# Two schedules of a two-block decoder kernel: the convolution stage projected by tokens, and the differential attention's steps behind later pieces

## The reference, cut to what matters

```python
def _odd_layer(h, w_in, conv_w, w_out, rows):          # convolution layer, width 4096 inside
    bg, cg, xt, g = jnp.split(h @ w_in, 4, axis=-1)    # w_in: 2048 x 16384
    y = bg * _conv3(cg * xt, conv_w, rows) * jax.nn.silu(g)
    return y @ w_out
# _conv3: three taps along each row of 64 tokens, zero at the row's ends
```

## Time and profile before

| | |
|---|---|
| runs | 2790.6, 2791.35 (median), 2792.13 us |
| profiled execution | 2791.76 us, its span 2790.1 us |
| busy share of the span | TensorE 96%, weight loads 90%, VectorE 63%, ScalarE 46%, GpSimd 1% |
| chain that ended last | TensorE 80%, VectorE 8%, ScalarE 4%, DMA 4%, VectorE's queue 3% |
| DMA | 534.59 MB, mean 192 GB/s |
| convolution stage | about 1847 to 2592 us of the span |
| differential attention | about 444 to 662 us, its last steps to 701 us |

### The profile page before, as it was taken

The page is one execution under the profiler, slowest core; times in us unless marked ns, Lnnn a source line. Parts: engine busy times, 40 slices in busy tenths (PEclk is TensorE's granted clock), DMA queues, the critical chain, the costliest instruction groups (busy, mean ns, idle before and its releaser), DMA issues.

```text
span 2790.1 us, 47619 instructions
## 1 busy us (share of the span) xinstructions
PE 2682.4 (96%) x18449; PEld 2500.2 (90%) x18449; DVE 1749.9 (63%) x2260; ACT 1278.6 (46%) x1702; POOL 18.4 (1%) x33
## 2 busy tenths in 40 slices
PE   7999999998899799999999999999999999999997
PEld 7999889998888699999989988889999999999886
DVE  6868878786875755545557545566775555555644
ACT  5557444555545444434443344444454444444443
POOL 1000000000000000000000000000000000000000
PEclk9999999999999899999999999999999999999999
DMA  6565866764566455655568645547875555556553
GB/s 190 147 200 167 277 185 197 221 204 142 187 213 213 155 179 173 194 163 184 175 194 265 205 144 181 191 152 235 282 256 183 180 187 174 188 173 195 175 201 138
DMA packets 450706, 534.59 MB, mean 192 GB/s; under 512 B 32955, under 2 KB 343750, under 8 KB 449670
## 3 DMA queue, kind: packets, MB, share of 16 engines
q1 hardware_dynamic: 447840, 522.29, 58.5%
q0 software_dynamic: 2064, 10.11, 1.2%
q10 hardware_dynamic: 662, 0.25, 0.0%
HBM read 530.46 MB, written 2.10 MB: 191 GB/s over the span
## 4 chain that ended last, share of the span: by engine, by line
PE 80%; DVE 8%; ACT 4%; DMA 4%; DVEq 3%; issue 1%; SPq 1%; ACTq 0%
PE banks L1802 15%; PE banks L1804 14%; PE banks L1803 14%; PE banks L1813 10%; PE banks L1814 10%; PE banks L1815 10%; DVE w_lo L1197 3%; DMA w_raw<-in_ev_w_in 2%; ACT w_hi L673 1%; PE banks L2195 1%; DVEq L1188 1%; PE banks L1965 1%; ACT scr_a L794 1%; DMA w_raw<-in_od_w_in 1%; SPq L492 1%
## 5 line engine op out<-in xcount | busy, mean ns | idle before, releaser
L1197 DVE TENSOR_TENSOR w_lo<-w_raw,w_hi 128x1024 fp32r<-128x1024 f32 (+2 forms) x848 | 974.4, 1160 | 744.2 <-ACT w_hi L673 723.1
L673 ACT ACTIVATE w_hi<-w_raw 128x1024 fp32r<-128x1024 f32 (+2 forms) x848 | 842.8, 1005 | 1012.4 <-PE banks L1815 394.6
L1802 PE MATMUL banks<-act_hl,w_hi 128*128 128x256 f32 x4048 | 1169.3, 289 | 37.5 <-DVE w_lo L1197 14.2
L1803 PE MATMUL banks<-act_hl,w_hi 128*128 128x256 f32 x4048 | 1149.9, 284 | 0.0
L1804 PE MATMUL banks<-act_hl,w_lo 128*128 128x256 f32 x4048 | 1149.7, 284 | 0.0
L1802 PEld LDWEIGHTS banks<-act_hl,w_hi 128*128 128x128 f32 x4048 | 780.4, 193 | 53.9 <-issue 21.7
L1803 PEld LDWEIGHTS banks<-act_hl,w_hi 128*128 128x128 f32 x4048 | 781.0, 193 | 1.9 <-issue 0.7
L1804 PEld LDWEIGHTS banks<-act_hl,w_lo 128*128 128x128 f32 x4048 | 780.5, 193 | 0.0
L1813 PE MATMUL banks<-w_hi,act_hl 128*128 128x512 f32 (+3 forms) x1376 | 510.5, 371 | 7.9 <-DVE w_lo L1197 5.7
L1814 PE MATMUL banks<-w_lo,act_hl 128*128 128x512 f32 (+3 forms) x1376 | 509.8, 370 | 0.0
L1815 PE MATMUL banks<-w_hi,act_hl 128*128 128x512 f32 (+3 forms) x1376 | 508.7, 370 | 0.0
(11 more groups left out here) (275 smaller groups left out, 1643.7 us busy)
## 6 DMA issues: line engine op xcount, KB each, us to landing
w_raw<-in_od_w_in SPq DMA_DIRECT2D x256, 512.0 KB, 3.9
w_raw<-in_ev_w_in SPq DMA_DIRECT2D x256, 256.0 KB, 3.8
w_raw<-in_l_w_in SPq DMA_DIRECT2D x96, 512.0 KB, 4.3
w_raw<-in_l_w_in SPq DMA_DIRECT2D x128, 256.0 KB, 3.2
ada_ring<-in_ada_w SPq DMA_DIRECT2D x128, 256.0 KB, 4.3
w_raw<-in_l_w_out SPq DMA_DIRECT2D x64, 512.0 KB, 5.0
y_mix<-in_ada_w SPq DMA_DIRECT2D x128, 256.0 KB, 3.3
const_b<-in_ada_w SPq DMA_DIRECT2D x128, 256.0 KB, 4.8
```

The source lines that it names most:

```text
L673: last = nc.scalar.activation(dst(w_hi[:, p % RING, :]), src(w_raw[:, p % RING, :]), ACT.Copy)
L1197: last = tt(dst(w_lo[:, p % RING, :]), src(w_raw[:, p % RING, :]), dst(w_hi[:, p % RING, :]).bitcast(F32), ALU.subtract)
L1802: mm(out, hi, a[:, kt, 0:T], start=start, stop=False, skip_group_check=True)
L1803: mm(out, hi, a[:, kt, T:2 * T], start=False, stop=False, skip_group_check=True)
```

## The change

The convolution stage is projected by tokens: banks 0 and 1 take [c | g] of token tile 0 and 1, banks 2 and 3 [b | x], each in matmuls of 512 columns whose moving operand is two blocks of 256 weight columns. Behind piece 2 ScalarE copies c and takes Silu of g for both token tiles; VectorE then multiplies banks 2 and 3 by them, which gives b times the gate and x times c by tokens. Behind piece 3 TensorE turns both products to features in eight transposes, into banks 4 and 5. Behind piece 8 VectorE applies the taps from bank 5, skipping the row ends in place of a zero border, and multiplies by bank 4. The `mix_pair` steps move from 8 to 10, and in out3 the last ones from 7 to 8. In differential attention the exponentials are cut into two heads behind piece 7 and two behind piece 8; the normalisation goes from 8 to 9, the transposes from 7 to 8, probT's copy from 10 to 11, the values from 9 to 10, the square from 12 to 13, its sum from 11 to 12, the root from 14 to 15. VectorE's steps behind 6, 14 and 15 stay.

```diff
@@ -308,7 +308,7 @@
     "four": ("gate", "folded", "cols", "cols_sb", "rows", "rows_sb", "o", "y"),
-    "conv": ("y",),
+    "conv": ("prod", "turned", "y"),
 }.items():
@@ -543,9 +543,8 @@
 four_e, four_o = view(scr_b[:, 1536:1792], 2, P), view(scr_b[:, 1792:2048], 2, P)
-conv_x, conv_g, conv_b, conv_y = (scr_b[:, 512 * n:512 * n + 512] for n in range(4))
-conv_c = scr_b[:, 2576:3088]
-conv_z = scr_b[:, 2048:2576].rearrange("p (b r n) -> p b r n", b=2, r=4)
+conv_gc, conv_prod = view(scr_b[:, 0:1024], TT, 512), view(scr_b[:, 1024:2048], TT, 512)
+conv_y = scr_b[:, 2048:2560]
 gate_rows = scr_b[:, 2560:4608]
@@ -860,17 +859,19 @@
             nc.scalar.activation(at_g, at_g, ACT.Silu).then_inc(s["gate"], 1)
-        if p == 6:
+        if p == 7:
             sc.wait_ge(s["max"], i + 1)
-            exps(dif_s, range(4), s["exp"])
-        if p == 10:
+            exps(dif_s, (0, 1), s["exp"])
+        if p == 8:
+            exps(dif_s, (2, 3), s["exp"])
+        if p == 11:
             sc.wait_ge(s["probT"], i + 1)
             copy(view(dif_t, 2, 384), PS[:, 4:6, 0:384]).then_inc(s["probT_sb"], 1)
-        if p == 12:
+        if p == 13:
             sc.wait_ge(s["o"], i + 1)
...
             nc.scalar.activation(dif_sq, bank(6), ACT.Square).then_inc(s["sq"], 1)
-        if p == 14:
+        if p == 15:
             sc.wait_ge(s["mean"], i + 1)
@@ -955,15 +956,12 @@
         if p == 2:
-            sc.wait_ge(s["y"], i + 1)
-            full(sc, "conv", i, 1)
-            copy(conv_b, bank(A)).then_inc(s_free, 1)
-            full(sc, "conv", i, 2)
-            copy(conv_x, bank(B)).then_inc(s_free, 1)
-            full(sc, "conv", i, 3)
-            copy(conv_c, bank(C)).then_inc(s_free, 1)
-            full(sc, "conv", i, 4)
-            nc.scalar.activation(conv_g, bank(3), ACT.Silu).then_inc(s_free, 1)
+            sc.wait_ge(s["prod"], i + 1)
+            for t in range(TT):
+                full(sc, "conv", i, 1 + t)
+                copy(conv_gc[:, t, T:2 * T], PS[:, t, 0:T])
+                last = nc.scalar.activation(conv_gc[:, t, 0:T], PS[:, t, T:2 * T], ACT.Silu)
+                last.then_inc(s_free, 1)
@@ -1129,7 +1127,7 @@
             conv(p, i)
-            if p == 8:
+            if p == 10:
                 mix_pair(i - 8)
@@ -1143,7 +1141,7 @@
             4: mixes("out3", 10),
-            7: [y_ready("conv"), *mixes("out3", 11)],
+            8: [y_ready("conv"), *mixes("out3", 11)],
             12: [lambda: gate_rows_copy(2)]}))
@@ -1429,8 +1427,8 @@
             scores_max(dif_s, range(4), causal, 4, s["max"])
-        if p == 8:
-            ve.wait_ge(s["exp"], i + 1)
+        if p == 9:
+            ve.wait_ge(s["exp"], 2 * i + 2)
@@ -1521,25 +1519,29 @@
         s = S["conv"]
-        if p == 3:
-            ve.wait_ge(s_free, all_left("conv", i))
+        if p == 2:
+            ve.wait_ge(s_free, bank_count("conv", i, 2))
+            ve.wait_ge(s["turned"], i + 1)
+            for t in range(TT):
+                full(ve, "conv", i, 3 + t)
+                last = tt(conv_prod[:, t, :], PS[:, 2 + t, :], conv_gc[:, t, :], ALU.mult)
+                last.then_inc(s_free, 1)
+            drain().then_inc(s["prod"], 1)
+        if p == 8:
+
+            ve.wait_ge(s["turned"], i + 2)
             rows = "p (b r n) -> p b r n"
-            z, v = conv_z, conv_y.rearrange(rows, b=2, r=4)
-            tt(z[:, :, :, 1:65], conv_c.rearrange(rows, b=2, r=4), conv_x.rearrange(rows, b=2, r=4),
-               ALU.mult)
-            drain()
-            for tap in (1, 0, 2):
+            z, v = PS[:, 5, :].rearrange(rows, b=2, r=4), conv_y.rearrange(rows, b=2, r=4)
+            for tap, src, dst in ((1, (0, 64), (0, 64)), (0, (0, 63), (1, 64)), (2, (1, 64), (0, 63))):
                 for b in range(2):
                     w = pcol(CONV3_W, 32 * tap + 2 * i + b)
-                    zs = z[:, b, :, tap:tap + 64]
+                    zs, vs = z[:, b, :, src[0]:src[1]], v[:, b, :, dst[0]:dst[1]]
                     if tap == 1:
-                        ts(v[:, b, :, :], zs, w, None, ALU.mult)
+                        ts(vs, zs, w, None, ALU.mult)
                     else:
-                        stt(v[:, b, :, :], zs, w, v[:, b, :, :], ALU.mult, ALU.add)
+                        stt(vs, zs, w, vs, ALU.mult, ALU.add)
                 drain()
-            tt(conv_y, conv_y, conv_b, ALU.mult)
-            drain()
-            tt(yt[:, ds(2 * i, 2), :], halves(conv_y), halves(conv_g), ALU.mult).then_inc(s["y"], 1)
+            tt(yt[:, ds(2 * i, 2), :], halves(bank(4)), halves(conv_y), ALU.mult).then_inc(s["y"], 1)
@@ -1580,6 +1582,8 @@
         ve.sem_inc(S[stage]["y"], 1)
+    for name in ("prod", "turned"):
+        ve.sem_inc(S["conv"][name], 1)
@@ -1690,10 +1694,6 @@
         norm(*norm5, range(4))
-
-    def clear_borders():
-        nc.vector.memset(conv_z, 0.0)
-        drain()
@@ -1770,9 +1770,9 @@
             conv(p, i)
-            if p == 8:
+            if p == 10:
                 mix_pair("out3", i - 8)
-        split("conv")(0, placed({**norm_steps(last_block, *norm5), 8: [clear_borders]}))
+        split("conv")(0, placed(norm_steps(last_block, *norm5)))
         for first, end in LOOPS["conv"][1:]:
@@ -1780,9 +1780,10 @@
             1: [lambda: mix_pair("out3", KT // 2 - 1)],
-            2: [step(conv, 3, COUNT["conv"] - 1), *mixes("out3", 8, 9)],
+            2: [step(conv, 2, COUNT["conv"] - 1), *mixes("out3", 8, 9)],
             4: mixes("out3", 10),
-            7: mixes("out3", 11),
+            6: [step(conv, 8, COUNT["conv"] - 1)],
+            8: mixes("out3", 11),
             9: [lambda: gate_diags(2, 80)]}))
@@ -1946,11 +1947,12 @@
+        blocks = [w[:, slot, 0:1024].rearrange("p (a b n) -> p b a n", a=2, b=2) for w in (w_hi, w_lo)]
         for b in range(4):
...
                 enter(stage, i, 1 + b)
-            for q in range(2):
-                r = features(half(b, q), slot, 256 * b + q * P, act, p, first and q == 0, last)
+            hi, lo = (w[:, 1 - b // 2, :, :] for w in blocks)
+            r = tokens_of(bank(b), hi, lo, act, p, b % 2, first, last)
             if last and b < 3:
@@ -2115,17 +2117,17 @@
             sets_scores(pairs, 4).then_inc(s["scores"], 1)
-        if p == 7:
+        if p == 8:
             te.wait_ge(s["prob"], i + 1)
...
             transposes([v[:, h, 0, :] for h in range(2)], 4).then_inc(s["probT"], 1)
-        if p == 9:
+        if p == 10:
             te.wait_ge(s["probT_sb"], i + 1)
...
             r.then_inc(s["o"], 1)
-        if p == 11:
+        if p == 12:
             te.wait_ge(s["sq"], i + 1)
@@ -2233,6 +2235,20 @@
+    def conv(p, i):
+        s = S["conv"]
+        if p == 3:
+
+            te.wait_ge(s["prod"], i + 2)
+            te.wait_ge(s["y"], i + 1)
+            for part in range(2):
+                for t in range(TT):
+                    for q in range(2):
+                        c = part * T + q * P
+                        r = nc.tensor.transpose(PS[:, 4 + part, q * T + t * P:q * T + (t + 1) * P],
+                                                conv_prod[:, t, c:c + P], ident[:, :])
+            r.then_inc(s["turned"], 1)
+
     def gates_rows(n):
@@ -2310,9 +2326,10 @@
         norm(5, x, first_columns, lambda: te.wait_ge(s_added, COUNT["out2"]))
-        stage_loop(te, "conv", run("conv"), none, nothing)
+        stage_loop(te, "conv", run("conv"), conv, nothing)
     if wanted("out3"):
-        stage_loop(te, "out3", run("out3"), none, placed({11: [lambda: gates_rows(2)]}))
+        n = COUNT["conv"] - 1
+        stage_loop(te, "out3", run("out3"), none, placed({3: [step(conv, 3, n)], 11: [lambda: gates_rows(2)]}))
```

## The result

| | us | ratio to the kernel before |
|---|---|---|
| before, beside it | 2790.97 (4 runs, 2790.11 to 2792.13) | |
| changed | 2761.21 (4 runs, 2759.15 to 2761.80) | 0.989 [0.9878, 0.9902] |
| predicted | 2757.5 (range 2752 to 2779) | |

The account below looks back on a forecast made before the run. The prediction took the convolution stage as bound by TensorE's issue and differential attention by TensorE with small holes. Convolution -27.9 and attention -6.4 make -34.3: 2791.76 - 34.3 = 2757.5 us, range 2752 to 2779.

Parts of the forecast that it names:

- 1. Matmuls: Convolution pieces: 12 matmuls of 512 columns replace 24 of 256, 2.72 us a piece instead of 2.88; -41.0 us.
- mixing or tile: Whether 0.2333 us per 512-column matmul goes with mixing tiles in a piece or with the stationary operand's tile; forecast chose tile.
- slower rate: Rival: convolution's 512-column matmuls take 0.2333 us, so the width gives only 20.5 us; 2778.0 us in all; 16%.
- Broken operand: Rival: a convolution matmul over two blocks costs as two of 256 columns, 0.240 us; 2798.5 us, slower; 4%.
- A fixed cost of nearly nothing: Rival: a matmul costs only 2.5 ns beyond its columns, so the width gives 7.7 us; 2790.8 us; 3%.
- 2. Transposes: Eight new TensorE transposes per unit behind piece 3, 0.109 us each, nothing waited for; +14.0 us.
- 3. Hand-over: Bank 0 is 0.53 us late before units 1, 6, 7, 8, behind ScalarE's copy, table load and Silu; +2.1 us.
- 4. VectorE: Convolution units with modulation sums: VectorE's shorter chain ends waits for weights, leaving the four units full; -2.7 us.
- Unit 0: Convolution's unit 0: normalisation paces VectorE and a shorter piece 7 arrives before its low half; +0.4 us.
- the 0.7 of the gap: The gap of 0.67 us at the third low half of the output stage after the convolution goes; -0.7 us.
- 5. Attention: Differential attention a piece later: gaps close in three loop units, -6.0 us; behind the last unit -0.4; together -6.4.
- The attention gives it back: Rival: the new gap behind the last attention unit and a half-clocked stretch eat the 6.4 us; 2763.9 us; 10%.

Follow-up runs that it names:

- experiment 3: Changed kernel with each convolution matmul of 512 columns issued as two of 256 into the halves of the bank; 2799.35 us, 1.0033.
- 7: Changed kernel with 32 unused bytes ahead of the first activation tile, moving both activation tiles by 32 bytes; 2767.44 us, 0.9921.
- 11: Changed kernel with 32 unused bytes ahead of the weight rings, moving weights and both activation tiles together; 2757.58 us, 0.9884.
- experiment 10: The kernel before, with only 32 unused bytes added ahead of the first activation tile; 2768.57 us, 0.9923.
- 5: Changed kernel with the convolution's weights landed by two DMAs a piece, so the moving operand is one unbroken block; 2758.40 us, 0.9886.
- 4: Changed kernel with the eight transposes of every unit issued twice into the same places; 2771.32 us, 0.9934.
- experiment 8: Changed kernel with one Silu of one column ahead of ScalarE's first convolution loop; 2756.33 us, 0.9875.
- experiment 1: The kernel before with only the differential attention's part of the change, the convolution stage as it was; 2783.22 us, 0.9974.
- 6: Changed kernel with 32 unused bytes a partition ahead of the second activation tile's region, so it starts on a multiple of 64; 2753.19 us, 0.9868.
- 9: Changed kernel with VectorE's last attention step moved behind the first low half of the unit after mla's first; 2760.96 us, 0.9888.
- 12: Changed kernel with activations 32 bytes off for 256-column feature stages, both tiles on 64 for conv and output stages, one early Silu; 2742.12 us, 0.9832.

## Why the prediction was right, point by point

**1. Matmuls: right, and for a reason it did not know.** 2.72 a piece, -41.0, and experiment 3 has -38.7 for the width alone. Most of the 2.3 between them is that at 2.88 a piece the transposes cost 0.86 a unit (46.94 - 46.08) and a hand-over 0.5 (47.42 - 46.94), where they cost 0.92 and 0.7 at 2.72. I took 2.72 because that stretch read the first tile. That was the right choice, but "mixing or tile" was not the cause: it is how the tile's address stands to that of the weights (7 and 11). Had the allocator set `act` 32 bytes further on, the same change would have met 2.80 a piece, and a kernel before it at 2.83: from the convolution's 729.7 (experiment 10) to 738.0 (experiment 7), a loss for this part of the change, the transposes costing 14.7 where the width saves some 7. The rival "slower rate" was a question of 32 bytes. "Broken operand": nothing (5). "A fixed cost of nearly nothing" falls with the 38.7 of experiment 3. The row that I leaned on for the broken operand, 0.117 in the earlier trace rows, was no plain comparison either: its `c_norm` lies in the region that starts 32 bytes past a multiple of 64, and 256 columns take 0.117 to 0.118 in experiments 7 and 10 too, where the operands stand 32 bytes apart.

**2. Transposes: the term was a little small.** +14.0 forecast; a unit shows +0.80 in piece 3 and 0.12 in the piece behind, 0.92, so 14.7. They start 0.109 apart as in the earlier trace rows, and a second eight cost 0.87, 0.109 each (4). The 0.05 above that is the return to the projection, the 0.31 between the first two matmuls behind them where 0.227 is normal. Nothing waited for the products.

**3. Hand-over: right in place and in lateness, small in price.** Units 1, 6, 7, 8 and only these, by ScalarE's Silu behind the load. With Y the start of the last piece (2157.62 ahead of unit 7) the rows above have the copy from Y + 1.17 to 1.53, the load to 2.82 and the Silu to 3.21, where the forecast had 1.16, 1.54, 2.83 and 3.21. TensorE starts 0.55 late, forecast 0.53, though the gap is shown as 0.39. What the sum left out is the restart: the piece behind takes 2.89 where 2.72 is normal. The two pieces (3.27 and 2.89) make 0.72, 2.9 in all against 2.1; experiment 8 gave back 3.0. The step that failed is that a late bank costs its lateness alone. The Trainium skill, "ScalarE: Activation LUTs", in What ACT_TABLE_LOAD costs, adds a drain of some 1.38 us to the load's 1.28; this trace shows none (copy over at 2159.15, Silu starting at 2160.45).

**4. VectorE: right.** Units 1 to 4 went from 190.3 to 181.4 us (1889.22 to 2070.64): the width makes it 4 x 16 x 0.16 = 10.2 less, the transposes 4 x 0.92 = 3.7 more and the stand ahead of unit 1 lengthens its first piece by 0.1, which leaves 2.5 for the waits that went. That size is good to about 1 us only: in experiment 1, with the convolution as before, the same four units took 189.2. Unit 0 cost 0.8 instead of 0.4, since its first piece (5.29, a matmul every 0.43) runs at the 1.2 GHz level. In out3 the 0.7 of the gap went and the last unit's transposes came, and the stage stayed as long as it was. The convolution and out3 together: -41.0 + 14.7 + 2.9 - 2.5 - 0.7 + 0.8 = -25.8, measured -26.0.

**5. Attention: the mechanism was right, and the sum by two errors that cancel.** Both gaps went from the three loop units, and with them 2.4 us a unit, not 2.0: the piece that stood 0.62 had been 0.78 longer than its neighbours (3.66 against 2.88), since a gap is shown too short by what the last matmul's busy time holds (0.28 where 0.12 is its cost). No gap came in their place. That is -7.2 in diff where -6.0 was forecast. Behind the last unit came 0.78 on the probabilities (forecast 1.1) and 4.75 on the low half (4.7), and in this trace the stretch at 1.2 GHz moved there; but mla and out1 together took 0.8 more, where -0.4 was forecast. Diff, mla and out1 make -6.4, the forecast to the tenth, and by luck: with the same steps experiments 1, 3 to 6, 8 and 11 have -5.5 to -6.9. "The attention gives it back" did not happen: a quarter of what diff gained went at most.

**The 3.7 us too low:** 0.5 is that the median of the changed kernel lies above its profiled execution. Of the other 3.2, hand-over has 0.8, transposes 0.7 and unit 0 0.4; the attention has none. Four and out2, which no part of the change touches and which vary in the other runs, took 1.5 more. These make 3.4; the last is the largest share, and it is inferred from those stages' spread, not traced to a cause.

## What to carry to other kernels

Count what wide matmuls save from two stretches of the same kernel, and look at the operands' addresses before naming a cause: one line of padding was worth 20 us here, two thirds of what the new schedule brought. A removed stand is worth more than the gap that the profile shows, 0.72 for 0.39: count it from start to start, and add the slow restart. Check a gain against stages that the edit leaves alone before calling it the edit's (1). Before moving a step that ends a chain, list everything that waits for the chain; what you free may only uncover the next (9).

## What the runs showed of the hardware

- **Placement of TensorE's two operands.** Only offsets of 0 and 32 bytes modulo 64 were tried, in fp32, full arrays, one weight load per matmul, in the stages below:

| operands' starts modulo 64 | 512 columns | 256 columns |
|---|---|---|
| the same (changed, 3, 6, 11) | 0.227 us | 0.120 |
| 32 apart (before's `act2`, 7, 10, 12) | 0.233 | 0.117 to 0.118 |

The sign turns between the widths; why is open. The table holds where one width follows itself. A piece of the context stage has three: 256 and 512 columns from `act`, 384 from `act2`. There the mean distances from start to start are 0.1183, 0.2323 and 0.1762 in the changed kernel, 0.1170, 0.2328 and 0.1771 in experiment 7, and 0.1183, 0.2310 and 0.1774 in 6. The 512 columns are at 0.232 though their operands start alike, which no run explains. And since what one width gains the others lose, the stage stayed at 469.1 to 469.3 in experiments 6, 7, 11 and 12; the 467.8 of 10 is open.

- **What a stand costs.** A gap in the profile starts where the last matmul's shown busy time ends, so it is short by 0.16: at 256 columns (0.28 shown, 0.12 apart) 0.62 costs 0.78, at 512 columns (0.39 shown, 0.227 apart) 0.39 is 0.55. At 512 columns the piece behind was 0.17 longer on top, with 0.34 between its first two matmuls.
- **A moving operand of two blocks with a hole** runs at the rate of one block (5).
- **One Silu ahead of the loop** removes sixteen table loads, two in each of the loop's eight passes, and brings one: L963 has 8 in the changed kernel and none in experiment 8, L672 17 and 9. That they stand in the loop's body because another table could be active on its entry is argued from this, not shown.
